# Feed-forward up: seven-product slots from 9 to 18 per layer, their weight sums moved mostly to Pool

## The reference, cut to what matters

```python
def conv_ffn(x, buf, p, l):
    u, buf_new = causal_conv(x @ p['ffn_w_up'][l], buf, p['ffn_conv_w'][l])
    u = u + p['ffn_conv_b'][l]
    return (jax.nn.silu(u[..., :D_FF]) * u[..., D_FF:]) @ p['ffn_w_down'][l], buf_new
```

## Time and profile before

| what | us |
|---|---|
| median of 3 runs (2887.61 to 2890.92) | 2889.76 |
| the profiled execution, its own time | 2890.29 |
| its span | 2888.6 |
| granted TensorE clock, share of full | 0.988 |
| TensorE busy | 2756.4 (95% of the span) |
| VectorE busy | 1524.4 (53%) |
| ScalarE busy | 1024.2 (35%) |
| Pool busy | 477.7 (17%) |

### The profile page before, as it was taken

How to read it: one execution, slowest core, us unless ns; L and a number is a source line. 1 busy time by engine, 2 the same in 40 slices (tenths; PEclk the granted TensorE clock), 3 DMA queues, 4 the chain that set the end, 5 groups by cost and what they waited for, 6 DMA issues and landing times. The chain is left out here.

```text
span 2888.6 us, 58689 instructions
## 1 busy us (share of the span) xinstructions
PE 2756.4 (95%) x22859; PEld 2195.5 (76%) x22859; DVE 1524.4 (53%) x3221; ACT 1024.2 (35%) x3105; POOL 477.7 (17%) x605
## 2 busy tenths in 40 slices
PE   7999999999999999999999899899998999999998
PEld 4779768898766667898766777668895679867887
DVE  7665547642243327753542565337726875537661
ACT  2233234522432224431655344325412133324431
POOL 0000110063213210054100002110161000110044
PEclk9999999999999999999999999999999999999998
DMA  5420124434333223343433004533442330123442
GB/s 155 155 75 6 40 71 146 132 127 116 87 108 91 72 78 119 130 132 116 138 104 109 6 6 122 162 113 128 132 137 77 122 105 6 27 68 121 131 136 78
DMA packets 356654, 287.82 MB, mean 100 GB/s; under 512 B 74700, under 2 KB 352764, under 8 KB 355996
## 3 DMA queue, kind: packets, MB, share of 16 engines
q1 hardware_dynamic: 337456, 267.03, 30.1%
q10 hardware_dynamic: 14828, 14.93, 1.6%
q0 software_dynamic: 4096, 2.11, 0.4%
HBM read 263.29 MB, written 20.73 MB: 98 GB/s over the span
## 5 line engine op out<-in xcount | busy, mean ns | idle before, releaser
L362 PE MATMUL bank<-h,weights 128*128 128x320 f32 (+2 forms) x3152 | 788.6, 408 | 8.1 <-ACT h L447 8.1
L362 PEld LDWEIGHTS bank<-h,weights 128*128 128x128 f32 (+1 forms) x3152 | 567.9, 189 | 217.3 <-issue 17.1
L362 PE MATMUL bank<-arena,weights 128*128 128x320 f32 (+5 forms) x3088 | 663.3, 375 | 12.2 <-DVE arena L1407 6.6
L362 PE MATMUL bank<-arena 128*128 128x160 f32 (+7 forms) x5034 | 640.1, 291 | 12.3 <-DVE arena L2745 5.1
L362 PEld LDWEIGHTS bank<-arena,weights 128*128 128x128 f32 (+2 forms) x3088 | 505.4, 188 | 153.3 <-issue 23.0
L362 PEld LDWEIGHTS bank<-arena 128*128 128x128 f32 (+2 forms) x5034 | 543.7, 171 | 37.1 <-issue 14.5
L571 POOL TENSOR_TENSOR arena<-weights 128x512 f32<-128x512 f32 (+1 forms) x48 | 58.2, 1212 | 726.6 <-DMA weights<-ffn_w_down 630.6
L362 PE MATMUL bank<-h,arena 64*64 64x64 f32 (+3 forms) x3000 | 174.4, 232 | 2.6 <-DVE h L1980 1.7
L1643 POOL TENSOR_TENSOR arena<-arena,consts 128x256 f32<-128x256 f32 x30 | 22.9, 765 | 829.1 <-DVE arena L1968 583.9
L362 PEld LDWEIGHTS bank<-h,arena 64*64 64x64 f32 (+1 forms) x3000 | 151.3, 143 | 7.9 <-DVE h L1980 2.8
L894 DVE SCALAR_TENSOR_TENSOR arena<-arena,params 128x336 f32<-128x336 f32 x176 | 105.7, 601 | 68.2 <-ACT arena L754 59.4
(11 more groups left out here) (373 smaller groups left out, 3697.5 us busy)
## 6 DMA issues: line engine op xcount, KB each, us to landing
weights<-ffn_w_up SPq DMA_DIRECT2D x88, 1024.0 KB, 5.1
weights<-ffn_w_down SPq DMA_DIRECT2D x32, 1024.0 KB, 5.4
weights<-rw_wrkv SPq DMA_DIRECT2D x24, 1024.0 KB, 5.2
weights<-gdn_w_in SPq DMA_DIRECT2D x24, 1024.0 KB, 5.4
arena<-cache_mla_latent SPq DMA_DIRECT2D x108, 128.0 KB, 2.3
weights<-ffn_w_down SPq DMA_DIRECT2D x16, 768.0 KB, 4.9
weights<-rw_wo SPq DMA_DIRECT2D x8, 1024.0 KB, 5.5
weights<-gdn_wo SPq DMA_DIRECT2D x8, 1024.0 KB, 5.8
```

The costliest lines, as they stand in the source:

```text
L362: return pe.matmul(out, lhsT, rhs, start=first, stop=last, skip_group_check=True)
```

## The change

FASTS becomes 4 to 21, all 18 slots, so nine more slots per layer are fast. Pool makes s1, s2 and s4 of every fast up slot; VectorE makes s3 of slot s + 1 in iteration s (`third_sum`). The gate is split in two: VectorE makes the products g * u for even s, and the multiplications by the sigmoid (with the mixes that follow from them) one iteration later, for odd s, or in the last iteration. GD gets two buffers in use. S1C alternates with s instead of s / 2, and waits on an earlier fast slot name slot s - 1 or s - 2 in place of s - 2 or s - 4.

```diff
--- before.py
+++ after.py
@@ -159,7 +159,6 @@
     "ffn_gate": "gate_gu hff",
     "fast_products": "m1 m2 m3 m4 m5 m6 m7 part_done",
     "fast_weights": "s1 s2 s3 s4",
-    "fast_weights_dve": "ds1 ds2 ds3 ds4",
     "fast_activations": "mix1 mix2 mix3 mix4",
     "fast_tiles": "u2 tt vv c11d c12 c21 c22",
     "fast_copies": "s1c c11",
@@ -546,7 +545,7 @@
         S1C, U2, TT, VV = [HALFSUM[:, i, :] for i in (0, 1)], HALFSUM[:, 2, :], HALFSUM[:, 3, :], HALFSUM[:, 4, :]
 
         UP = [(c, half) for c in range(11) for half in range(2)]
-        FASTS = range(4, 21, 2)
+        FASTS = range(4, 22)
         summed = [key for l in range(layers) for key in
                   [("up", l, UP[s][1], UP[s][0]) for s in FASTS] + [("down", l, c, part) for c in range(4) for part in range(3)]]
         sum_of = {key: i for i, key in enumerate(summed)}
@@ -571,7 +570,8 @@
             eng.tensor_tensor(s1, a21, a22, ALU.add).then_inc(*to(made["m5"], key))
             eng.wait_ge(*at(made["m5"], key))
             eng.tensor_tensor(s2, s1, a11, ALU.add).then_inc(*to(made["m6"], key))
-            eng.tensor_tensor(s3, a11, a21, ALU.add).then_inc(*to(made["m7"], key))
+            if made["m7"] == "s3":
+                eng.tensor_tensor(s3, a11, a21, ALU.add).then_inc(*to("s3", key))
             eng.wait_ge(*at(made["m6"], key))
             eng.tensor_tensor(s4, s2, a12, ALU.add).then_inc(*to(made["m3"], key))
 
@@ -597,8 +597,8 @@
                     "m5": (s1, lambda k: mix[:, 0, k, :]), "m6": (s2, lambda k: mix[:, 1, k, :]),
                     "m7": (s3, lambda k: mix[:, 2, k, :])}
 
+        UP_SUM = {"m6": "s2", "m5": "s1", "m7": "ds3", "m3": "s4"}
         POOL_SUM = {"m6": "s2", "m5": "s1", "m7": "s3", "m3": "s4"}
-        DVE_SUM = {"m6": "ds2", "m5": "ds1", "m7": "ds3", "m3": "ds4"}
         MIX_FOR = {"m6": "mix2", "m5": "mix1", "m7": "mix3", "m4": "mix4"}
 
         def pe_fast_up(pe, l, c, half):
@@ -619,8 +619,8 @@
                 else:
                     ps = of(("fd", key))[:, 0:HN]
                     pe.wait_ge(*at("c22", key))
-                if step in DVE_SUM:
-                    pe.wait_ge(*at(DVE_SUM[step], key))
+                if step in UP_SUM:
+                    pe.wait_ge(*at(UP_SUM[step], key))
                 if step in MIX_FOR and (c, half) == UP[FASTS[0]]:
                     pe.wait_ge(*at(MIX_FOR[step], ("up", l)))
                 a, b = ops[step]
@@ -785,9 +785,9 @@
                 if s in FASTS:
                     key = slot_key(l, s)
                     act.wait_ge(*at("m1", key))
-                    if s - 4 in FASTS:
-                        act.wait_ge(*at("u2", slot_key(l, s - 4)))
-                    act.activation(S1C[s // 2 % 2], of(("fa", key))[:, 0:HN], ACT.Copy).then_inc(*to("s1c", key))
+                    if s - 2 in FASTS:
+                        act.wait_ge(*at("u2", slot_key(l, s - 2)))
+                    act.activation(S1C[s % 2], of(("fa", key))[:, 0:HN], ACT.Copy).then_inc(*to("s1c", key))
                 if s >= 1:
                     tails(s - 1)
                 if 2 <= s < len(UP) and s not in FASTS:
@@ -846,6 +846,8 @@
 
         def pool_ffn(pool, l):
             pool.wait_ge(*at("rstd", 4 * l + 2))
+            for s in FASTS:
+                half_sums(pool, slot_key(l, s), UP_SUM)
             for c in range(4):
                 for part in range(3):
                     half_sums(pool, ("down", l, c, part), POOL_SUM)
@@ -866,18 +868,21 @@
             dve_mixes(dve, [UMIX[:, i] for i in range(4)], H[:, 0:4, :], H[:, 4:8, :], ("up", l))
             dve.wait_ge(*at("xp_zero", l))
 
-            def gate(m):
+            def gate_products(m):
 
                 g, u = CONV[:, 0, m % 2, :], CONV[:, 1, m % 2, :]
                 dve.wait_ge(*at("conv", (l, 1, m)))
-                if m:
-                    dve.wait_ge(*at("hff", (l, m - 1)))
-                dve.tensor_tensor(GD[:, 0, :], g, u, ALU.mult).then_inc(*to("gate_gu", (l, m)))
+                if m >= 2:
+                    dve.wait_ge(*at("hff", (l, m - 2)))
+                dve.tensor_tensor(GD[:, m % 2, :], g, u, ALU.mult).then_inc(*to("gate_gu", (l, m)))
+
+            def gated(m):
+
                 dve.wait_ge(*at("gate_gu", (l, m)))
                 dve.wait_ge(*at("gate_s", (l, m)))
-                s = EGATE[:, m % 2, :]
-                dve.tensor_tensor(HFF[:, m, 0:SEQ], GD[:, 0, 0:SEQ], s[:, 0:SEQ], ALU.mult)
-                win = [ap[:, 256:336].rearrange("p (b w) -> p b w", b=DEC)[:, :, 2:10] for ap in (GD[:, 0, :], s)]
+                gu, s = GD[:, m % 2, :], EGATE[:, m % 2, :]
+                dve.tensor_tensor(HFF[:, m, 0:SEQ], gu[:, 0:SEQ], s[:, 0:SEQ], ALU.mult)
+                win = [ap[:, 256:336].rearrange("p (b w) -> p b w", b=DEC)[:, :, 2:10] for ap in (gu, s)]
                 dve.tensor_tensor(sample(HFF[:, m, SEQ:NT]), win[0], win[1], ALU.mult).then_inc(*to("hff", (l, m)))
 
             def conv(n):
@@ -887,6 +892,7 @@
                 dve.wait_ge(*at("tap2", (l, half, m)))
                 if half == 0 and m >= 2:
                     dve.wait_ge(*at("gate_e", (l, m - 2)))
+                    dve.wait_ge(*at("gate_gu", (l, m - 2)))
                 if n:
                     dve.wait_ge(*at("conv", (l, order[n - 1][1], order[n - 1][3])))
                 for step in xp_ready(l, n):
@@ -897,6 +903,14 @@
                 dve.scalar_tensor_tensor(out=CONV[:, half, m % 2, :], in0=XP[:, n % 4, 0:336], scalar=w(0),
                                          in1=CT[:, 2, :], op0=ALU.mult, op1=ALU.add).then_inc(*to("conv", (l, half, m)))
 
+            def third_sum(key):
+
+                (a11, _, a21, _), (_, _, s3, _) = quarters(key)
+                dve.wait_ge(*at(f"slot{where[key] % NS}", key))
+                if sum_of[key] >= NSUM:
+                    dve.wait_ge(*at(*weight_used[summed[sum_of[key] - NSUM]]))
+                dve.tensor_tensor(s3, a11, a21, ALU.add).then_inc(*to("ds3", key))
+
             def last_half(n, done, key, ps, add, op):
 
                 for step in conv_users(l, n):
@@ -910,37 +924,41 @@
                 conv(2 * s - 2)
                 if key:
                     fb, fc, fd = (of((name, key)) for name in ("fb", "fc", "fd"))
-                    if s - 2 in FASTS:
-                        dve.wait_ge(*at("c21", slot_key(l, s - 2)))
+                    if s - 1 in FASTS:
+                        dve.wait_ge(*at("c21", slot_key(l, s - 1)))
                     dve.wait_ge(*at("m6", key))
                     dve.wait_ge(*at("s1c", key))
-                    dve.tensor_tensor(U2, fb[:, 0:HN], S1C[s // 2 % 2], ALU.subtract).then_inc(*to("u2", key))
+                    dve.tensor_tensor(U2, fb[:, 0:HN], S1C[s % 2], ALU.subtract).then_inc(*to("u2", key))
                 conv(2 * s - 1)
                 if key:
                     dve.wait_ge(*at("m5", key))
                     dve.wait_ge(*at("u2", key))
-                    if s - 2 in FASTS:
-                        dve.wait_ge(*at("c12", slot_key(l, s - 2)))
+                    if s - 1 in FASTS:
+                        dve.wait_ge(*at("c12", slot_key(l, s - 1)))
                     dve.tensor_tensor(TT, fc[:, 0:HN], U2, ALU.add).then_inc(*to("tt", key))
                     dve.wait_ge(*at("m7", key))
                     dve.wait_ge(*at("tt", key))
                     last_half(2 * s + 1, "c22", key, fd, TT, ALU.add)
                 if s + 1 in FASTS:
-                    half_sums(dve, slot_key(l, s + 1), DVE_SUM)
+                    third_sum(slot_key(l, s + 1))
                 if s % 2 == 0:
-                    gate(s - 2)
-                    gate(s - 1)
+                    gate_products(s - 2)
+                    gate_products(s - 1)
+                if s % 2 and s > 1 or s == len(UP):
+                    pair = s - 2 if s == len(UP) else s - 3
+                    gated(pair)
+                    gated(pair + 1)
                 if key:
                     dve.wait_ge(*at("m3", key))
                     last_half(2 * s, "c12", key, fb[:, HN:NT], TT, ALU.subtract)
                     dve.wait_ge(*at("m4", key))
                     dve.tensor_tensor(XP[:, (2 * s + 1) % 4, 2:2 + HN], fd[:, 0:HN], U2, ALU.add).then_inc(*to("c21", key))
-                if s % 2 == 0 and s // 2 - 1 in MIXED:
-                    part, a, b = MIXED[s // 2 - 1]
+                if (s % 2 and s > 1 or s == len(UP)) and pair // 2 in MIXED:
+                    part, a, b = MIXED[pair // 2]
                     k0, kp = DOWN_ROWS[part][0], DOWN_ROWS[part][1] // 2
-                    dve.wait_ge(*at("hff", (l, s - 1)))
+                    dve.wait_ge(*at("hff", (l, pair + 1)))
                     dve_mixes(dve, [DMIX[part][:, i, a:b] for i in range(4)], HFF[:, k0 + a:k0 + b, :],
-                              HFF[:, k0 + kp + a:k0 + kp + b, :], ("down", l, part, s // 2 - 1))
+                              HFF[:, k0 + kp + a:k0 + kp + b, :], ("down", l, part, pair // 2))
```

## The result

| | median (lowest to highest), us | ratio to the kernel before (95%) |
|---|---|---|
| before, same chip | 2889.26 (2887.61 to 2890.92), 4 runs | |
| after | 2919.55 (2917.80 to 2920.38), 4 runs | 1.0109 (1.0096 to 1.0121) |

The profiled execution took 2920.18, its span 2918.5. The forecast was 2893, "no change", with a range that ended at 2917: the kernel is slower where no change was forecast, and its time lies 2.6 us above the range.

What follows compares the result with a forecast made beforehand. TensorE was taken to bound the up stage (busy 145.9 of 147 us). -36.3 (faster slots) + 43.6 (new stalls) - 4.2 (old slot 20 stalls) = +3.1 on the profiled 2890.29: 2893.4, "no change", range 2867 to 2917.

Steps and rivals of the forecast that it cites:

- (1) TensorE: Up stage: nine more slots in each of 4 layers go from 8.61 to 7.61 us, -36.3 us.
- The turns: VectorE operations with two SBUF inputs alternate with Pool's sums, each waiting for a running one; a turn costs 1.13 us.
- (3) Even slot without mixes: Fast up slots: c22 ends 6.23 us into the slot, in time by 0.23, so no stall.
- The slower rival: Pool wins one more turn at the slot's head, ordinary even slots stall 0.9 each: 2922 us; chance 0.36.
- (3) Mixed slots: Up slots 8, 10, 16, 18, with mixes before their taps: m4 2.05 us late each, 8.2 per layer.
- the walk: Step-by-step timing of VectorE's and Pool's operations through one fast up slot, giving when c22 ends and m4 starts.
- (3) Odd slots: Up slots 5, 7, 13, 15, taps behind ScalarE's sigmoids: m4 0.35 us late each, 1.4 per layer.
- (3) Slots 20 and 21: End of the up stage, Pool making four sums for the down product: 0.65 us late each, 1.3 per layer.
- (3): Pool making three sums per fast up slot: VectorE's delay before c22 stalls TensorE 10.9 us per layer, +43.6 in all.
- (4) The last block: Gates and mixes of tiles 20, 21 end before part 2 of the first down block: covered, at most 7 us.

Runs made afterwards that it cites:

- e2: Changed kernel with Pool's three sums of every up slot replaced by memsets of the same 512 columns, which read no SBUF; 2858.72 us, ratio 0.9882.
- e1: Changed kernel with Pool's three sums 2 columns wide instead of 512 in slots 7 to 21 of each layer; 2868.37 us, ratio 0.9916.
- e7: Changed kernel with Pool making the sums of slots 5 and 6 only after c22 of slot 4; 2923.6 us, ratio 1.0128.
- e11: e3 with Pool's first two sets of down sums waiting for c21 of slots 20 and 21; 2921.74 us, ratio 1.0126.
- e13: e11 with Pool making s1 and s2 of odd slots, VectorE all other up sums; 2908.53 us, ratio 1.0067.
- e4: Changed kernel with Pool also making the third sum of slot 4; 2919.76 us, ratio 1.0091.
- e9: Changed kernel with slots 4, 8, 10, 16 and 18 normal, so 13 fast slots per layer; 2920.88 us, ratio 1.0099.
- e6: Changed kernel with Pool beginning the sums of slot s + 2 only after c22 of slot s, first two down-sum sets likewise; 2973.88 us, ratio 1.0297.
- e15: e13's split with slots 4 to 20 fast, 21 normal, and only the second set of down sums held back; 2883.3 us, ratio 0.9981.
- e3: Changed kernel with all four weight sums of an up slot on VectorE, Pool idle until the down sums; 2906.35 us, ratio 1.0045.

## Why the prediction was wrong

- **(1) TensorE, -36.3:** right, by e2.
- **The turns:** right, and shown by e1 and e2. A tap behind a Pool sum ends 0.37 after it, as in the earlier trace rows, a mix 0.35.
- **(3) Even slot without mixes, no stall:** right, 0 in slots 6, 12 and 14. c22 was to end 6.23 into the slot; slot 6 starts at 468.84 and c22 (L919) ends at 475.08, 6.24.

```profile
474.87 0.21 DVE L919 TENSOR_TENSOR arena<-bank,small 128x64 f32<-128x64 f32 x1
```

- **The slower rival**, Pool winning one more turn at the head, gave 2922, near the result, but did not happen: slots 6, 12 and 14 are where it would show. That its number is close is an accident.
- **(3) Mixed slots, 2.05:** 2.17, right to 0.12. Nearly all of that is a thing the walk left out: the 8 passes behind a stall take 1.19 from start to start, not 1.09 (483.48 to 484.67 above).
- **(3) Odd slots, 0.35:** 0.62. m4 came 7.04 into slot 7, not 6.87. VectorE's first two taps, U2 and Pool's sums are within 0.03 of the walk; from U2 to the tap behind it I took the 0.24 of the earlier trace rows, an even slot, and here it is 0.37 (the walk's m4 is 0.17 early, 0.13 of it by this). The 0.10 of the passes comes on top.

```profile
481.17 0.31 DVE L931 TENSOR_TENSOR small<-bank,small 128x160 f32<-128x160 f32 x1
481.54 0.57 DVE L900 SCALAR_TENSOR_TENSOR arena<-arena,params 128x336 f32<-128x336 f32 x1
```

- **(3) Slots 20 and 21, 0.65:** 0.78, and 1.1 in one layer.
- **The step that failed** is the sentence of (3), "It works two slots ahead and is about 4 us long, so TensorE never waits for Pool; I cost that at nothing". TensorE does not wait for a Pool sum in the steady slots. But at the head of the stage Pool makes three slots' sums in a row, and they stand against taps that VectorE must do before `third_sum`: seven of its first eight take 1.4 to 1.6. Slot 4 was costed 0 and lost 12.5 in four layers. e2 (no loss there) and e7 (3.1 to 0.63) show the cause; e1 (14.2 lost in slot 4 with its half clock, as in the changed kernel) shows that Pool's sums of slots 7 and later have no part in it.
- **The clock** was costed at nothing, in no sentence at all: 5.1 here. It comes after the stalls: e1, which has no stall in slots 7 to 18, has no such stretch there and still has those in slot 4 of layers 2 and 3; e2 has none in its up stages.
- **(4) The last block, covered:** right, the first down block is as long as before (20.9). How much room is left was not measured; e11 and e13 show that down sums which wait for c21 cost 6 to 9 us a layer there.

The 25.3 by which 68.9 exceeds 43.6 are 12.5 (slot 4), 5.1 (clock), 3.5 (odd), 2.2 (mixed), 1.7 (slots 20, 21) and 0.3. The rest of the kernel, outside the feed-forwards, adds 2, which is within what differs there from one execution to the next.

Three of my own moves (e4, e7, e9) removed or shortened the stall that they aimed at, and e6 freed the taps that it aimed at; each made others as large or larger: I walked the operations in question, and not what stands behind them. What stays open is whether some order of VectorE's work brings 18 slots below e15; splitting the mixes over two iterations was not tried.

## What to carry to other kernels

Price work that runs on Pool beside VectorE by the number of turns, up to about 1.1 us for each Pool sum of this size, and not by the columns of the VectorE operation that waits; then moving three short sums to Pool can cost VectorE more than making them (e3 against the change). Walk the first slots of a stage by themselves, where the helper engine runs ahead without a brake, and the last ones, where the next stage's work begins. Add to each stall what comes after it: 0.1 us here, and up to 1.7 where the granted clock fell.

## What the runs showed of the hardware beyond that

- A 64-column operation with two SBUF inputs takes 0.22 us alone and 1.28 behind a Pool sum (e3, e6); a 160-column one 1.40 and 1.43 (e13), against 1.75 for 512 columns (e15).
- Pool memsets of 128x512 take 0.53 and don't delay such operations (0.48 beside them, e2).
- The granted clock fell to 0.50 for 3.4 us inside a stage at 0.99, after 3.00 us of which TensorE was busy 1.47. The same stall in slots 8, 10 and 16 brought none in any layer, so a stall of that size is not enough by itself. Which slot has the stretch differs between runs: in e4 it came in slot 16 of layer 0 and not in slot 18.
